# Two attention stages that walk their heads in pairs, with matmuls that alternate between halves of the array

## The reference, cut to what matters

```python
# stage ab: heads 0-7 (4 query heads share a key head), width 64
logits = einsum('bqgrd,bkgd->bgrqk', qb, k) * 64 ** -0.5
o_a = softmax(logits) @ v
# stage ab: heads 8-15, width 64, a learned bias by distance
logits = einsum('bqhd,bqkhd->bhqk', qb, kg) * 64 ** -0.5 + bias
# stage mla: 16 heads, 64 + 32 = 96 wide queries and keys, 64 wide values
logits = (q_n @ k_n + q_r @ k_r) * 96 ** -0.5
p = softmax(logits); o_c = p @ v
# both: h = h + concat(heads) @ w_out
```

## Time and profile before

| | |
|---|---|
| median of 3 runs | 1608.7 us (1602.38 to 1620.78) |
| the profiled execution, its own time | 1601.97 us |
| its span, first to last instruction | 1600.2 us |
| busy: TensorE matmul, its weight loads | 96%, 92% |
| busy: VectorE, ScalarE, GpSimd | 63%, 48%, 26% |
| mean granted TensorE clock | 0.981 of full speed |
| 16 heads and the first output chunk, ab | 1050.94 to 1106.30 us |
| the same in mla | 1342.48 to 1396.90 us |

### The profile page before, as it was taken

How to read it: one execution, slowest core, us unless ns; L and a number is a source line. 1 busy time by engine, 2 the same in 40 slices (tenths; PEclk the granted TensorE clock), 3 DMA queues, 4 the chain that set the end, 5 groups by cost and what they waited for, 6 DMA issues and landing times.

```text
span 1600.2 us, 31973 instructions
## 1 busy us (share of the span) xinstructions
PE 1535.4 (96%) x13406; PEld 1476.9 (92%) x13406; DVE 1015.0 (63%) x998; ACT 768.5 (48%) x1007; POOL 414.8 (26%) x392
## 2 busy tenths in 40 slices
PE   9999985999999999999899999999999988999997
PEld 8999985999999999999799999967999987699997
DVE  7767768575566756575575567446766675476665
ACT  6444531454444544476554435655434356553433
POOL 2999925010002000057320001754000033410000
PEclk9999997999999999999999999999999998999999
DMA  7555553445454555545155554431555541145552
GB/s 270 188 207 183 207 114 112 167 171 209 182 208 171 216 201 183 195 168 180 73 185 203 192 186 182 168 110 64 200 185 183 209 160 52 41 183 200 183 208 79
DMA packets 54822, 271.20 MB, mean 169 GB/s; under 512 B 17680, under 2 KB 22032, under 8 KB 23344
## 3 DMA queue, kind: packets, MB, share of 16 engines
q1 hardware_dynamic: 53648, 266.58, 46.6%
q0 software_dynamic: 1088, 3.38, 0.7%
HBM read 266.52 MB, written 3.42 MB: 169 GB/s over the span
## 4 chain that ended last, share of the span: by engine, by line
PE 84%; DVE 7%; ACT 2%; POOL 2%; issue 2%; DMA 1%; SPq 1%; DVEq 0%; POOLq 0%; ACTq 0%
PE ps L658 78%; PE ps L994 2%; PE ps L984 2%; DVE xlo L1526 2%; DVE wlo L1520 1%; PE ps L972 1%; DVE h L1542 1%; DMA uP<-turned_u 1%; ACT whi L1135 1%; ACT pm L1397 0%; POOL pm L523 0%; DVE ps L1739 0%; PE ps L930 0%; POOL rinv L522 0%; POOL sq L467 0%
## 5 line engine op out<-in xcount | busy, mean ns | idle before, releaser
L1520 DVE TENSOR_TENSOR wlo<-raw,whi 128x2048 fp32r<-128x2048 f32 x245 | 572.2, 2338 | 230.3 <-ACT whi L1135 230.0
L1135 ACT CAST whi<-raw 128x2048 fp32r<-128x2048 f32 x245 | 468.4, 1913 | 253.4 <-PE ps L658 241.2
L658 PE MATMUL ps<-xhi,whi 128*128 128x256 f32 x2048 | 570.4, 279 | 7.1 <-DVE xlo L1526 4.1
L658 PE MATMUL ps<-xlo,whi 128*128 128x256 f32 x2048 | 567.6, 277 | 0.0
L658 PE MATMUL ps<-xhi,wlo 128*128 128x256 f32 x2048 | 567.5, 277 | 0.0
L658 PEld LDWEIGHTS ps<-xhi,whi 128*128 128x128 f32 x2048 | 386.3, 189 | 10.7 <-DVE xlo L1526 3.2
L658 PEld LDWEIGHTS ps<-xlo,whi 128*128 128x128 f32 x2048 | 386.3, 189 | 0.0
L658 PEld LDWEIGHTS ps<-xhi,wlo 128*128 128x128 f32 x2048 | 386.2, 189 | 0.0
L658 PE MATMUL ps<-hhi,whi 128*128 128x256 f32 x1216 | 335.7, 276 | 0.0
L658 PE MATMUL ps<-hlo,whi 128*128 128x256 f32 x1216 | 335.6, 276 | 0.0
L658 PE MATMUL ps<-hhi,wlo 128*128 128x256 f32 x1216 | 335.6, 276 | 0.0
(11 more groups left out here) (244 smaller groups left out, 1935.6 us busy)
## 6 DMA issues: line engine op xcount, KB each, us to landing
raw<-in_wstream SPq DMA_DIRECT2D x245, 1024.0 KB, 4.8
raw<-in_wstream SPq DMA_DIRECT2D x4, 512.0 KB, 7.3
h<-in_xT SPq DMA_DIRECT2D x4, 256.0 KB, 5.8
turned_u<-sq SPq DMA_DIRECT2D x8, 128.0 KB, 4.6
uP<-turned_u SPq DMA_DIRECT2D x8, 128.0 KB, 3.3
turned_y<-gs SPq DMA_DIRECT2D x8, 128.0 KB, 2.1
sq<-turned_y SPq DMA_DIRECT2D x16, 64.0 KB, 2.4
biasA<-bias_rows POOLq DMA_DIRECT2D x5, 192.0 KB, 5.2
```

Source lines behind the costliest of these rows:

```text
L658: return pe.matmul(o, l, r, start=first, stop=last, skip_group_check=True)
L1135: act.copy(whi[:, slot, :], raw[:, slot, :]).then_inc(S("whi_ready"), 1)
L1520: dve.tensor_tensor(wlo[:, slot, :], raw[:, slot, :], whi[:, slot, :], ALU.subtract)\
```

## The change

Both stages call new functions, one for each engine, that walk eight pairs of heads. The scores of a pair go to banks 0 and 1 or 6 and 7, and their four matmuls alternate between the two heads: in ab between partitions 0 to 63 and 64 to 127 of the array's rows, in mla between two tiles of 96 rows each. The four matmuls of `pv` alternate between the two heads and so between columns 0 to 63 and 64 to 127. `pm` and `pT` have four buffers, two of them in the space of `tk` and `tsq`, and `mx`, `nmx`, `rs`, `rinv` four columns; `lg` keeps two. Scores run two pairs ahead of the transposes. GpSimd takes one reciprocal for a pair and waits for both heads' exponentials. Of the pairs without a bias VectorE copies the odd head's transposes. Parts of the output projection stand between the last pairs' work for both halves of the outputs, and after the last `pv` tiles 3 to 6 come ahead of tile 7. In mla the split of the weight chunk moves from the stage's end to the fourth pair. The moba stage keeps its order. Indentation is cut by 12 or 8 below, and the removed lines of `attention` that served only these two stages are left out.

```diff
-mx = [sb(f"mx{b}", [P, TT]) for b in range(2)]
-nmx = [sb(f"nmx{b}", [P, TT]) for b in range(2)]
-rs = [sb(f"rs{b}", [P, TT]) for b in range(2)]
-rinv = [sb(f"rinv{b}", [P, TT]) for b in range(2)]
+mx = sb("mx", [P, 4, TT])
+nmx = sb("nmx", [P, 4, TT])
+rs = sb("rs", [P, 4, TT])
+rinv = sb("rinv", [P, 4, TT])
...
+pm4 = pm + [sb(f"pm{2 + b}", [P, TT, T], where=tk_at + 2048 * b) for b in range(2)]
+pT4 = pT + [sb(f"pT{2 + b}", [P, TT, T], where=tk_at + 4096 + 4096 * b) for b in range(2)]
...
+SCORE_BANKS = (0, 1, 6, 7)
...
+def normalise_pairs(st):
+    for p in range(KT):
+        b = slice(2 * (p % 2), 2 * (p % 2) + 2)
+        pool.wait_ge(S(st + "_exp"), 4 * p + 4)
+        chain(pool.tensor_tensor(rinv[:, b, :], rs[:, b, :],
+                                 power[:, 1:2].unsqueeze(2).to_broadcast([P, 2, TT]), ALU.pow))
+        for s in (2 * p, 2 * p + 1):
+            x = pm4[s % 4]
+            pool.tensor_tensor(x[:, :, :], x[:, :, :],
+                               rinv[:, s % 4, :].unsqueeze(2).to_broadcast([P, TT, T]), ALU.mult)\
+                .then_inc(S(st + "_pn"), 1)
...
-normalise("ab")
+normalise_pairs("ab")
...
+def attention_pairs(st, o_banks):
+    F, hs = FIRST[st], HEADS[st]
+    FO = F + len(TOK[st]) + (3 if st == "mla" else 0)
+    def scores(p):
+        if p >= 2:
+            pe.wait_ge(S(st + "_exp"), 4 * (p - 1))
+        for t in range(TT):
+            for s in (2 * p, 2 * p + 1):
+                last = pe.matmul(ps[:, SCORE_BANKS[s % 4], t * T:(t + 1) * T],
+                                 hs[s]["q"][:, t * P:(t + 1) * P], hs[s]["k"][:, 0:T],
+                                 start=True, stop=True, skip_group_check=True)
+                if t == TT - 1:
+                    last.then_inc(S(st + "_sc"), 1)
+    def turn(s):
+        pe.wait_ge(S(st + "_pn"), s + 1)
+        if s >= 2:
+            pe.wait_ge(S(st + ("_ptc_even", "_ptc_odd")[s % 2]), s // 2)
+        for kt in range(TT):
+            for t in range(TT):
+                last = pe.transpose(ps[:, 2 + s % 2, kt * T + t * P:kt * T + (t + 1) * P],
+                                    pm4[s % 4][:, t, kt * P:(kt + 1) * P], ident)
+        last.then_inc(S(st + "_pt"), 1)
+    def pv(p):
+        pe.wait_ge(S(st + "_ptc_even"), p + 1)
+        pe.wait_ge(S(st + "_ptc_odd"), p + 1)
+        if p >= 2:
+            pe.wait_ge(S(st + "_olo"), p - 1)
+        for kt in range(TT):
+            for s in (2 * p, 2 * p + 1):
+                hd = hs[s]
+                last = pe.matmul(ps[hd["row"]:hd["row"] + 64, 4 + p % 2, 0:T],
+                                 vtok[:, kt, hd["v"]:hd["v"] + 64], pT4[s % 4][:, kt, :],
+                                 start=kt == 0, stop=kt == TT - 1, skip_group_check=True)
+        last.then_inc(S(st + "_pv"), 1)
+    def out_part(m, k0, k1):
+        slot = FO % NSLOT
+        w = slice(m * P, (m + 1) * P)
+        for k in range(k0, k1):
+            pe.wait_ge(S(st + "_olo"), k + 1)
+            last = mm3(half_bank(o_banks[0], m), whi_b[slot][:, k, w], wlo_b[slot][:, k, w],
+                       yhi[:, k, :], ylo[:, k, :], k == 0 and m == 0, k == KT - 1)
+        return last
+    if st == "mla":
+        pe.wait_ge(S("mla_qTc"), 8)
+        pe.wait_ge(S("mla_knc"), 8)
+        pe.wait_ge(S("mla_vc"), 4)
+        pe.wait_ge(S("mla_krs"), 1)
+    else:
+        pe.wait_ge(S(st + "_rowT"), sum(c["dst"] is not None for c in TOK[st]))
+        pe.wait_ge(S(st + "_evac"), sum(c["v"] is not None for c in TOK[st]))
+        pe.wait_ge(S("bvec_ready"), 1)
+    scores(0)
+    scores(1)
+    for p in range(KT):
+        if p + 2 < KT:
+            scores(p + 2)
+        turn(2 * p)
+        if p >= 1:
+            pv(p - 1)
+        turn(2 * p + 1)
+        if p == KT - 2:
+            chunk_ready(FO, None)
+            out_part(0, 0, 3)
+        if p == KT - 1:
+            out_part(1, 0, 3)
+    pv(KT - 1)
+    out_part(0, 3, 7)
+    out_part(1, 3, 7)
+    out_part(0, 7, 8)
+    out_part(1, 7, 8).then_inc(S("w_used"), 1)
+    for q in range(1, 4):
+        proj(FO + q, None, o_banks[q], operand=(yhi, ylo))
...
+def attention_pairs(st):
+    F, hs = FIRST[st], HEADS[st]
+    def exponents(s):
+        hd = hs[s]
+        act.wait_ge(S(st + "_nmx"), s + 1)
+        if s >= 4:
+            act.wait_ge(S(st + "_pt"), s - 3)
+        for t in range(TT):
+            if hd["bias"] is None:
+                src, sc = ps[:, SCORE_BANKS[s % 4], t * T:(t + 1) * T], hd["scale"]
+            else:
+                src, sc = lg[s % 2][:, t, :], 1.0
+            act.activation(pm4[s % 4][:, t, :], src, ACT.Exp, scale=sc, bias=nmx[:, s % 4, t:t + 1],
+                           accum_out=rs[:, s % 4, t:t + 1]).then_inc(S(st + "_exp"), 1)
+    def turned(s):
+        act.wait_ge(S(st + "_pt"), s + 1)
+        if s >= 4:
+            act.wait_ge(S(st + "_pv"), s // 2 - 1)
+        dst = pT4[s % 4][:, :, :]
+        if hs[s]["bias"] is None:
+            turned_copy = act.copy(dst, bank2(2 + s % 2))
+        else:
+            turned_copy = act.copy(dst.rearrange("p m (t c) -> p (m t) c", t=TT), reversed_tiles(bank2(2 + s % 2)))
+        turned_copy.then_inc(S(st + ("_ptc_even", "_ptc_odd")[s % 2]), 1)
+    def out_high(p):
+        act.wait_ge(S(st + "_pv"), p + 1)
+        act.copy(yhi[:, p, :], ps[:, 4 + p % 2, 0:T]).then_inc(S(st + "_ohi"), 1)
+    for s in range(4):
+        exponents(s)
+    for p in range(KT):
+        turned(2 * p)
+        if p + 2 < KT:
+            exponents(2 * p + 4)
+        if p >= 1:
+            out_high(p - 1)
+        if hs[2 * p + 1]["bias"] is not None:
+            turned(2 * p + 1)
+        if p + 2 < KT:
+            exponents(2 * p + 5)
+        if st == "mla" and p == 3:
+            split_hi(F + len(TOK[st]) + 4)
+    out_high(KT - 1)
     out_projection(st, F + len(TOK[st]) + (3 if st == "mla" else 0))
...
+def attention_pairs(st, o_banks):
+    F, hs = FIRST[st], HEADS[st]
+    def maxima(s):
+        hd, b = hs[s], s % 4
+        bank = SCORE_BANKS[b]
+        dve.wait_ge(S(st + "_sc"), s + 1)
+        if s >= 4:
+            dve.wait_ge(S(st + "_exp"), 2 * (s - 3))
+        src, scale = bank2(bank), hd["scale"]
+        if hd["bias"] is not None:
+            i = hd["bias"]
+            if hd["n_bias"] == 0:
+                dve.wait_ge(S("bias_loaded"), 128)
+            else:
+                dve.wait_ge(S(st + "_exp"), 2 * (s - 1))
+            row_ = biasA[:, i, :] if i < 5 else biasB[:, i - 5, :]
+            for t in range(TT):
+                dve.scalar_tensor_tensor(out=lg[s % 2][:, t, :], in0=ps[:, bank, t * T:(t + 1) * T],
+                                         scalar=scale, in1=row_[:, P - P * t:P - P * t + T],
+                                         op0=ALU.mult, op1=ALU.add).then_inc(S(st + "_lg"), 1)
+            dve.wait_ge(S(st + "_lg"), 2 * hd["n_bias"] + 2)
+            src, scale = lg[s % 2][:, :, :], 1.0
+        chain(dve.reduce_max(mx[:, b, :], src, AX.X))
+        dve.tensor_scalar(nmx[:, b, :], mx[:, b, :], -scale, None, ALU.mult).then_inc(S(st + "_nmx"), 1)
+    def turned_odd(s):
+        dve.wait_ge(S(st + "_pt"), s + 1)
+        if s >= 4:
+            dve.wait_ge(S(st + "_pv"), s // 2 - 1)
+        dve.tensor_copy(pT4[s % 4][:, :, :], bank2(3)).then_inc(S(st + "_ptc_odd"), 1)
+    def out_low(p):
+        dve.wait_ge(S(st + "_ohi"), p + 1)
+        dve.tensor_tensor(ylo[:, p, :], ps[:, 4 + p % 2, 0:T], yhi[:, p, :], ALU.subtract)\
+            .then_inc(S(st + "_olo"), 1)
+    for s in range(4):
+        maxima(s)
+    for p in range(KT):
+        if p + 2 < KT:
+            maxima(2 * p + 4)
+            maxima(2 * p + 5)
+        if hs[2 * p + 1]["bias"] is None:
+            turned_odd(2 * p + 1)
+        if p >= 1:
+            out_low(p - 1)
+        if st == "mla" and p == 3:
+            split_lo(F + len(TOK[st]) + 4)
+    out_low(KT - 1)
     out_projection(st, F + len(TOK[st]) + (3 if st == "mla" else 0), o_banks)
...
-attention("ab", (6, 7, 0, 1))
+attention_pairs("ab", (0, 1, 6, 7))
```

More of the change, by code:

```diff
@@ L1116, in _ @@
             mla_up()
-            attention("mla", (6, 7, 0, 1))
+            attention_pairs("mla", (0, 1, 6, 7))
             mlp("mlp1")
@@ L1369, in attention @@
                             act.wait_ge(S(st + "_pv"), m - 1)
[L1370 to L1377, removed]
+                        act.copy(pT[m % 2][:, 0, :], half_bank(2 + m % 2, 0))
+                        act.copy(pT[m % 2][:, 1, P:T], half_bank(2 + m % 2, 1)[:, P:T]).then_inc(S(st + "_ptc"), 1)
                     if 0 <= s - 3 < n:
@@ L1392, in attention @@
                             w = n_keys(hd, t)
[L1393 to L1398, removed]
+                            act.activation(pm[b][:, t, 0:w], lg[b][:, t, 0:w], ACT.Exp, bias=nmx[:, b, t:t + 1],
+                                           accum_out=rs[:, b, t:t + 1]).then_inc(S(st + "_exp"), 1)
@@ new lines, in attention @@
+                out_projection(st, F + len(TOK[st]) + (3 if st == "mla" else 0))
```

(22 more changed lines are left out.)

11 lines of the change are left out of this document (6 added, 5 removed).

## The result

The kernel with pairs takes 1597.66 us (median of 20 runs, 1589.42 to 1602.10), the kernel before, run beside it, 1606.82 (20 runs, 1600.67 to 1620.78): ratio 0.9928, interval 0.9912 to 0.9944. That is 9 to 14 us, where 22 to 23 were forecast, and under the 1% that the forecast gave as the line. The profiled execution took 1592.3 us, its span 1590.4, with 0.982 of the full clock on average.

What follows compares the result with a forecast made beforehand. TensorE was taken to bound both stages, and TensorE and the weight stream the rest. ab -12.5 and mla -9.4 gave -21.9 us: 1580.1 from the profiled execution, 1586.8 from the median, forecast 1584 between them, range 1573 to 1601.

Steps and rivals of the forecast that it cites:

- Small things: One reciprocal fewer per pair and a second semaphore lie beside other work; the rest of the kernel keeps its order.
- Rival 5: Both stages: TensorE, streaming less, stays at half clock through 12 pairs; +17 us, 1620, slower by 1%; chance 0.05.
- 1: VectorE and GpSimd set the pace all through, `nmx` hitting `pm` more often; -17.5 us, so 1588; chance 0.16.
- 2: Scores and `pv`: halves abreast but half a step late, 8 records in 5 steps; -18.5 us, 1587; chance 0.08.
- 3: ab: row halves don't overlap, column halves do; -18.5 us, 1587; chance 0.07.
- 4: Both stages: nothing overlaps, and each alternation pays for a change of form; some +7 us, 1613; chance 0.12.
- The forecast -12.5: ab: -16.4 us on TensorE, +3.3 for VectorE, +1.5 at the start, -0.9 at the end.
- -16.4 + 3.3: ab: TensorE pairs of 3.27 us instead of 5.32 save 16.4; four pairs waiting for VectorE give back 3.3.
- The 4.1 us for a pair with a bias: ab: VectorE's time for two heads with a bias and a `ylo` (3.6 to 4.7), against TensorE's 3.27.
- The forecast -9.4: mla: -10.0 us from TensorE pairs of 3.77 instead of 5.02, +1.5 at the start, -0.9 at the end.
- The split: mla, fourth pair: TensorE waits 2 to 3 us, about as much as was idle before; nothing (1 gained to 1.5 lost).
- The best bounds together: Both stages: no loss at the starts, 1.3 for VectorE, 1 gained at the split; given as -27.6 us.

Runs made afterwards that it cites:

- e4: Pairs in mla alone, with ab keeping the old attention of the kernel before; 1606.14 us, ratio 0.9982.
- e8: The kernel with pairs, but a pair's scores and `pv` matmuls issued head after head instead of half by half; 1598.38 us, a single execution.
- e7: The kernel with pairs, plus a second settling matmul one third of a loop body later in mlp0 and mlp1; 1581.82 us, ratio 0.9845.
- e5: The kernel with pairs, with the settling matmul issued twice in a row ahead of the loops of mlp0 and mlp1; 1577.73 us, ratio 0.9825.

## Why the prediction was right or wrong

The range (1573 to 1601) holds the 1597.66, the forecast of 1584 is 13.7 too low, and the gain stayed within 1%, to which the text gave 0.25.

**The step that failed** is the last sentence of "Small things", "The rest of the kernel keeps its order; it is bound by TensorE and by the stream of weights", taken as: its time stays too. The order stayed and TensorE stayed the bound, but its matmuls came 4% further apart in the two loops behind the changed stages, 13.2 us. No rival had it. Rival 5 asked for the clock, and the granted clock was 1.00 in these loops. That the range held is luck: its slow end was there for rivals 1 to 4, and what used it up was none of them.

**ab.** The forecast -12.5 is -12.50. By parts: from the first transpose to the last `pv` 45.48 us before and 32.61 after, -12.9 (forecast -16.4 + 3.3 = -13.1); from the first score to the first transpose 5.09 and 6.32, +1.2 (forecast +1.5); from the last `pv` to the end of the first output chunk 4.79 and 3.92, -0.9 (forecast -0.9). Rows of s5 were the right ones for halves that differ in rows alone. The 4.1 us for a pair with a bias came out otherwise: the four steps in which VectorE prepares such a pair (from `pv` to `pv`, starting with the second) took 4.04, 4.94, 4.61 and 3.74. `nmx` had a mean of 0.49 us, between the two stretches of the earlier trace rows, and 1.0 where it met a `pm`. And a term was missing: since scores run two pairs ahead, the copies of pairs 3 and 4, which have no bias, fall into the steps of the first two pairs with one, another 0.69 us on VectorE in each. Together that is 17.3 us against the forecast's 16.4; that the whole part is 0.2 off all the same is luck in part. GpSimd's reciprocal of four columns takes 1.01 us, not 0.7.

**mla.** The forecast -9.4 was -11.5. Its pair is 3.77 us to the digit. The split was put at nothing, by "about as much was idle at the end". In truth both were larger: before, the chain has TensorE out of it from 1382.45 to 1388.91, 6.5 us, after the last scores, with the 1.89 us reciprocal beside `wlo` of the earlier trace rows; after, the split cost 3.6 us with the half clock that it brought. The start lost 0.95 (forecast 1.5), 2.6 in e4. From the last `pv` to the end of the first output chunk it gained 0.9, as forecast.

**The rivals.** 1 holds in the steps with a bias only: in the others of ab, and in mla but for the split, no pair waits for VectorE. 2 to 4 fall with eight records in 1.06 us; in e8 even the order that 2 argued about changes nothing, and the starts of its records aren't in program order between the two halves. 5 happened for a short time, in the 4 us behind the split.

**The sums.** The best bounds together give -27.9, not -27.6. Rival 5's +17 us, put between the low end and the median as the forecast was, is 1623, not 1620. Neither changes the range or a chance.

**Shown and argued.** Shown: the loops' pace is one of two and changes only at a restart (e7 turns it in mid-stage, e5 by one matmul); it isn't the pairs' work as such, since e5 has it too. Argued, from the spacings alone: that a few nanoseconds in which the stream resumes choose the pace. Not excluded for the mlp stages: the place of their code. The test, a settling matmul a few columns wider, wasn't tried. Nor is it known why the pairs lead to the pattern 120 215 307.

## What to carry to other kernels

Price a change in its own stage from the rows there, and then compare, behind it, the number of matmuls in 100 us of the loops that it left alone: a busy share of 100% and a full clock don't say that a stream has kept its pace. A sum that is right in its stages can be half given back there, and one idle-looking instruction at a restart can be worth more than a rewritten stage, though as a draw, not as a rule. And put long instructions of ScalarE and VectorE where nothing that TensorE needs is queued behind them: here moving the split three pairs later gave 3.6 us. How much of that was the queue and how much `pm` held by `wlo`, no run separates.

## What was not expected of the hardware

- A stream of fp32r matmuls of 256 columns runs at 113.3 or at 117.8 ns per matmul, at the same granted clock (1.00), and keeps the pace for up to 175 us, across iterations, until the stream is interrupted.
- Executions of one kernel differ in it, which is part of their scatter: ffn2 is slow in one execution of before (1608.54 us) and fast in another (1601.97).
- Float32 halves lie abreast even when they are issued head after head (e8): a record of the second head starts ahead of three that are issued before it.
- `nmx` of 0.17 us is held for 1.00 us by a `pm`, and a `pm` of 1.0 us for 3.09 by `wlo`.
- A wait of 1.96 us with TensorE busy around it was followed by a stretch at 0.57 of the clock.
